# A two-layer hybrid encoder step on one core: reordering ahead of the sliding-window attention, an earlier key split, and a feed-forward loop written out

## The reference

```python
h = rms_norm(x, ln_mix)
qa, ka, va, fa, qb, kb, vb = split(h @ w_in)     # 8 heads x 64 with forgetting; 8 q / 2 kv heads x 64 windowed
logf = log_sigmoid(fa + b_f)                     # decay per head: cumsum(logf)
o = concat(fox(qa, ka, va, cumsum(logf)),        # causal softmax(q k / 8 + c_q - c_k) v
           swa(rope(qb), rope(kb), vb, sinks))   # own chunk of 64 and two before it, a sink per head
x = x + o @ w_out                                # 1024 -> 1024
x = x + cross_attend(rms_norm(x), mem)           # 4 heads x 128 into 256 memory tokens
gate, val = split(rms_norm(x) @ w_up)            # 2 x 2816
x = x + (silu(causal_conv3(gate)) * val) @ w_down
```

## Time and profile before

| | |
|---|---|
| median of 3 runs | 3662.82 us (3659.05 to 3664.21) |
| profiled execution, own time | 3655.24 us |
| its span | 3653.4 us |
| mean granted TensorE clock | 0.968 of full |
| PE busy | 3391.1 us (93%) |
| DVE, POOL, ACT busy | 51%, 33%, 23% |
| HBM traffic | 46 GB/s over the span |

### The profile page before, as it was taken

The page is one execution under the profiler, slowest core; times in us unless marked ns, Lnnn a source line. Parts: engine busy times, 40 slices in busy tenths (PEclk is TensorE's granted clock), DMA queues, the critical chain, the costliest instruction groups (busy, mean ns, idle before and its releaser), DMA issues. The chain is left out here.

```text
span 3653.4 us, 52717 instructions
## 1 busy us (share of the span) xinstructions
PE 3391.1 (93%) x21112; PEld 3257.3 (89%) x21112; DVE 1879.3 (51%) x3464; ACT 835.7 (23%) x1872; POOL 1201.9 (33%) x976
## 2 busy tenths in 40 slices
PE   6999997889999999999989999979989999999997
PEld 6988897778889999999978988878888999999997
DVE  5443444777664444443644443457766443444345
ACT  4331231434320000000232322224443100000001
POOL 4113112433343333333432122124233333333331
PEclk9999998999999999999999999988999999999998
DMA  4112112111111111111121111111111111111111
GB/s 145 39 43 58 42 37 64 56 43 39 30 41 44 43 45 44 44 46 45 41 70 51 39 42 59 46 43 61 44 35 32 41 44 44 44 44 44 45 44 63
DMA packets 85396, 175.65 MB, mean 48 GB/s; under 512 B 10416, under 2 KB 13744, under 8 KB 84752
## 3 DMA queue, kind: packets, MB, share of 16 engines
q1 hardware_dynamic: 71968, 132.90, 12.8%
q10 hardware_dynamic: 13184, 39.23, 3.7%
HBM read 150.36 MB, written 16.29 MB: 46 GB/s over the span
## 5 line engine op out<-in xcount | busy, mean ns | idle before, releaser
L613 POOL TENSOR_TENSOR WH<-RAW,zero 128x512 fp32r<-128x512 f32 x484 | 544.9, 1126 | 2366.1 <-PE PS L633 2353.6
L633 PE MATMUL PS<-HH,WH 128*128 128x384 f32 (+1 forms) x3312 | 872.0, 336 | 101.3 <-POOL WL L615 19.5
L633 PE MATMUL PS<-HL,WH 128*128 128x384 f32 (+1 forms) x3312 | 853.3, 330 | 0.0
L633 PE MATMUL PS<-HH,WL 128*128 128x384 f32 (+1 forms) x3312 | 852.6, 329 | 0.0
L633 PEld LDWEIGHTS PS<-HH,WH 128*128 128x128 f32 x3312 | 592.8, 190 | 123.4 <-POOL WL L615 22.5
L615 POOL TENSOR_TENSOR WL<-RAW,WH 128x512 fp32r<-128x512 f32 x484 | 661.4, 1367 | 37.9
L633 PEld LDWEIGHTS PS<-HL,WH 128*128 128x128 f32 x3312 | 595.4, 190 | 0.0
L633 PEld LDWEIGHTS PS<-HH,WL 128*128 128x128 f32 x3312 | 592.8, 189 | 0.0
L1686 DVE TENSOR_TENSOR XT<-PS,XT 128x320 f32<-128x320 f32 x448 | 303.3, 719 | 269.5 <-PE PS L633 269.3
L633 PE MATMUL PS<-G0H,WH 128*128 128x384 f32 (+1 forms) x960 | 288.1, 349 | 45.4 <-DVE XT L1530 29.4
L1115 ACT ACTIVATE PTH<-PS 128x512 fp32r<-128x512 f32 (+4 forms) x320 | 165.5, 520 | 681.3 <-PE PS L633 680.2
(11 more groups left out here) (249 smaller groups left out, 5087.9 us busy)
## 6 DMA issues: line engine op xcount, KB each, us to landing
RAW<-in_slabs SPq DMA_DIRECT2D x484, 256.0 KB, 2.7
XR<-decays ACTq DMA_DIRECT2D x16, 512.0 KB, 5.8
XT<-in_xT SPq DMA_DIRECT2D x8, 544.0 KB, 8.1
XR<-decays ACTq DMA_DIRECT2D x16, 272.0 KB, 7.0
out_fk<-T ACTq DMA_DIRECT2D x8, 544.0 KB, 2.7
out_fv<-T ACTq DMA_DIRECT2D x8, 544.0 KB, 2.8
out_y<-YT ACTq DMA_DIRECT2D x8, 544.0 KB, 3.2
RX<-ST ACTq DMA_DIRECT2D x16, 136.0 KB, 2.4
```

Of the source, the lines that this page charges most:

```text
L613: pool.tensor_tensor(WH[:, s, :], RAW[:, s, :], zero[:, 0:1].to_broadcast([128, HALF]), ALU.add).then_inc(w_hi, 1)
L633: ins = pe.matmul(*a, **k)
```

## The change

It has these parts.

1. At a layer's start VectorE evicts key pair 0 before it waits for `ln_done`, and ScalarE copies `KH` right after the log-sigmoid, ahead of the decay transfers. `FZ` and `FA` move to the place of `QH` and `QL`.
2. The squares of the memory tokens (layer 0) become one ScalarE instruction and one `tensor_reduce` on VectorE in place of 8 and 7.
3. Ahead of the sliding-window run the projections go query 1, values, query 2, query 3, with the value transposes in two halves behind query 2 and query 3. The first half of ("out", 1), output tiles 0 to 3, is a block of its own (`down`) before the run. The other 12 parts go one to a step into gaps 0 and 2 of steps 0 to 11. All rotary embeddings are done before the run, each after the eviction of a projection and not before it; all but query 0's swaps go through `RX`, and VectorE copies `XKL` in place of ScalarE.
4. The feed-forward loop is a Python loop, so the five turns are straight code. `repeat`, `Silent` and `wait_apart` are gone, with the constant waits of each group and step; one wait on `const_ok` stays.

```diff
-    order += [("wq", 1), ("wq", 2), "wv", ("wq", 3), ("win", 0), ("out", 1, 0), ("out", 1, 1), ("win", 1)]
+    order += [("wq", 1), "wv", ("wq", 2), ("wq", 3), ("out", 1, 0), ("win", 0), ("out", 1, 1), ("win", 1)]
@@ swa_fill
-            fox, own = down_parts(("out", 1), G_ROWS), down_parts(("out", 2), WINDOW_ROWS)
+            fox, own = down_parts(("out", 1), G_ROWS)[12:], down_parts(("out", 2), WINDOW_ROWS)
-            fill = {-1: spread(fox[:1], (2,)), 11: spread(fox[-1:], (0, 1, 2))}
-            fill |= {s: spread(fox[2 * s + 1:2 * s + 3], (0, 1, 2)) for s in range(11)}
+            fill = {s: spread(fox[s:s + 1], (0, 2)) for s in range(12)}
@@ TensorE
                 project(pe, ("wq", 1), HH, HL, CH)
+                own = project(pe, "wv", HH, HL, CH)
                 project(pe, ("wq", 2), HH, HL, CH)
-                own = project(pe, "wv", HH, HL, CH)
+                value_tiles(pe, T32, V_GROUPS[:2], own_values, own)
                 project(pe, ("wq", 3), HH, HL, CH)
+                value_tiles(pe, T32, V_GROUPS[2:], own_values, own)
                 pe.wait_ge(o_free, place.at("step", 1))
-                attention(pe, swa_steps(), swa_fill(), {-1: lambda: value_hook(pe, own)})
+                down(pe, G_ROWS, [("out", 1, 0)])
+                attention(pe, swa_steps(), swa_fill(), {})
...
-                repeat(pe, place, (FT // 2 - 1) // 2, mixer)
+                for turn in range((FT // 2 - 1) // 2):
+                    mixer(pe, turn)
@@ ScalarE, layer start
                 act.activation(FA[:], FA[:], ACT.Ln, bias=one[0:8, :]).then_inc(ln_done, 1)
+                filled(act)
+                hi(act, [(KH[:], T32[:])])
@@ ScalarE, ahead of the run
                 hi(act, [(KH[:], XR[:, 2, :])])
+                filled(act)
+                rope_swap(act, STAGES[0], 0)
                 act.wait_ge(roped, place.at("rope", 2))
                 hi(act, [(QH[:], QLS)])
...
+                filled(act)
+                act.wait_ge(roped, place.at("rope", 3))
+                rope_swap(act, STAGES[1], 0)
+                value_groups(act, V_GROUPS[:2], own_rows)
+                filled(act)
+                act.wait_ge(roped, place.at("rope", 4))
+                rope_swap(act, STAGES[2], 0)
+                for h in range(2):
+                    ins = copy(act, XKH[64 * h:64 * h + 64], KH[64 - 64 * h:128 - 64 * h, :])
+                ins.then_inc(keys_ready, 1)
+                value_groups(act, V_GROUPS[2:], own_rows)
...
                 window_queries(1)
                 window_queries(2)
+                window_queries(3)
@@ VectorE, layer start
+                fill(dve, T32)
                 dve.wait_ge(ln_done, place.at("layer", 1))
...
-                fill(dve, T32)
                 keys()
@@ VectorE, ahead of the run
                 rope(dve, T32[:], 0, 0, XR[:, 2, :])
+                fill(dve, STAGES[0], stored=False)
                 rope(dve, QLS, 1, 0, QLS)
                 lo(dve, [(KL[:], XR[:, 2, :], KH[:])]).then_inc(low_keys, 1)
                 wait_own(dve, lo(dve, [(QL[:], QLS, QH[:])]))
                 sample_queries(dve, *WINDOW_Q[0])
-                fill(dve, STAGES[0], stored=False)
+                fill(dve, T32)
+                place.add("store")
                 rope(dve, STAGES[0], 0, 1, STAGES[0])
                 fill(dve, STAGES[1], stored=False)
-                rope(dve, STAGES[1], 1, 1, STAGES[1])
-                fill(dve, T32)
-                place.add("store")
+                value_groups(dve, V_GROUPS[:2], own_rows)
+                rope(dve, STAGES[1], 0, 2, STAGES[1])
                 dve.wait_ge(k32_out, place.at("layer", 16, 16))
                 fill(dve, STAGES[2], stored=False)
+                dve.wait_ge(low_keys, place.at("layer", 1))
+                for h in range(2):
+                    ins = dve.tensor_copy(XKL[64 * h:64 * h + 64], KL[64 - 64 * h:128 - 64 * h, :].bitcast(F32))
+                ins.then_inc(keys_ready, 1)
+                value_groups(dve, V_GROUPS[2:], own_rows)
+                add_out(dve, 0)
                 low_queries(1)
-                wait_own(dve, low_queries(2))
+                add_out(dve, 1)
+                low_queries(2)
+                add_out(dve, 2)
+                rope(dve, STAGES[2], 0, 3, STAGES[2])
+                add_out(dve, 3)
+                wait_own(dve, low_queries(3))
...
-                hooks |= {4: lambda: rope(dve, STAGES[2], 0, 2, STAGES[2]), 5: lambda: low_queries(3)}
-                hooks[-1] = own_values
@@ the memory tokens' squares
-                for m in range(KT):
-                    act.activation(MSQ[m][:], MR[:, m, :], ACT.Square).then_inc(msq_ready, 1)
+                act.activation(MSQ[:, :, :], MR[:, :, :], ACT.Square).then_inc(msq_ready, 1)
...
+                dve.tensor_reduce(MACC[:], MSQ[:].rearrange("p k n -> p n k"), mybir.AxisListType.X, ALU.add).then_inc(msq_used, 1)
```

More of the change, by code:

```diff
@@ L11 @@
-from contextlib import ExitStack, contextmanager
+from contextlib import ExitStack
 import numpy as np
@@ L66, in __init__ @@
         self.n = dict.fromkeys(self.KINDS, 0)
-        self.loops = []
     def at(self, kind, more=0, scale=1):
[L70 to L74, removed]
+        return self.n[kind] * scale + more
     def bank_set(self):
@@ L79, in set_count @@
     def set_count(self, more=0):
[L80 to L84, removed]
-    def uses_of(self, s, more=0):
[L88 to L92, removed]
+        return self.n["use"] // 2 + more
+    def uses_of(self, s, more=0):
+        return (self.n["use"] + 1 - s) // 2 + more
     def add(self, kind, k=1):
         self.n[kind] += k
[L98 to L132, removed]
 def slab_places():
@@ L745, in down @@
                 slots = None
-                for m in range(KT):
+                for m in range(4 * len(keys)):
                     s = claim(pe)
@@ L904, in scores @@
                     qh, ql = WINDOW_Q[st["pair"]]
-                    pe.wait_ge(keys_ready, place.at("layer", 2, 2))
+                    pe.wait_ge(keys_ready, place.at("layer", 3, 3))
                     for h in range(2):
@@ L915, in scores @@
                     kv = st["pair"] // 2
-                    pe.wait_ge(keys_ready, place.at("layer", 1, 2))
+                    pe.wait_ge(keys_ready, place.at("layer", 1, 3))
                     product(o + KEEP, DEC, QSH[:], QSL[:], KSH[:, kv, :], KSL[:, kv, :])
@@ L1306, in biases, with keys @@
                         act.dma_start(XR[64 * h:64 * h + 64, 2, :], row[:, SEQ:N_C8].to_broadcast([64, T])).then_inc(bias_in, 16)
-                def keys(pair, ready):
-                    ready(act)
+                def keys(pair):
+                    parts_filled(act)
                     hi(act, [(KH[:], T32[:])])
@@ L1316, in trig, with own_rows @@
                     act.dma_start(XR[:, 1, :], sin_t).then_inc(trig_in, 16)
+                def own_rows(tile):
+                    return 128 if tile < NB else DEC
                 biases(0)
-                keys(0, filled)
+                store_t32(act, o_fk[l * PAIRS], 0, T)
                 filled(act)
@@ L1377, in window_queries @@
                     hi(act, [(WINDOW_Q[p][0], STAGES[p - 1])])
-                filled(act)
                 window_queries(1)
                 window_queries(2)
-                for out, src in ((XKH, KH), (XKL, KL)):
-                    for h in range(2):
-                        ins = copy(act, out[64 * h:64 * h + 64], src[64 - 64 * h:128 - 64 * h, :])
-                ins.then_inc(keys_ready, 1)
+                window_queries(3)
+                place.add("use", KT // 2)
+                place.add("third", KT // 2)
                 def memory_tokens():
@@ L1450, in mixer @@
                         down(act)
-                repeat(act, place, (FT // 2 - 1) // 2, mixer)
+                for turn in range((FT // 2 - 1) // 2):
+                    mixer(act, turn)
                 act.dma_start(o_cv[l], CO[:]).then_inc(co_out, 16)
@@ L1632, in attention @@
                             waits.append((p_used, place.at("step", s + 1)))
-                        wait_apart(dve, memset_ok, 4, waits)
+                        for produced in waits:
+                            dve.wait_ge(*produced)
                         if st["kind"] == "swa":
@@ L1871, in mixer @@
                         down(dve)
-                repeat(dve, place, (FT // 2 - 1) // 2, mixer)
+                for turn in range((FT // 2 - 1) // 2):
+                    mixer(dve, turn)
                 if l < DEPTH - 1:
```

57 lines of the change are left out of this document (26 added, 31 removed).

## The result

The changed kernel takes 3581.15 us (median of 4 runs, 3576.0 to 3587.93), the kernel before 3661.03 (4 runs): ratio 0.9783, 95% interval 0.9767 to 0.9799, 79.9 us less. Its profiled execution has a span of 3574.2 us, 79.2 less than that of before; the mean granted clock rose from 0.968 to 0.977. The forecast was 3587, range 3569 to 3609.

What follows compares the result with a forecast made beforehand. It took TensorE as the bound, busy 3391.1 of 3653.4 us, gains coming only from idle time and half clock; -22.0 - 36.4 - 15.5 - 2 = -75.9 from 3655.24, plus 7.6 for the median: 3587 us, range 3569 to 3609.

Steps and rivals of the forecast that it cites:

- Feed-forward, -15.5: Feed-forward loop: the jump back idles TensorE 1.8 us at each of 8 returns, plus 1.1; straight code saves 15.5 us.
- rival 2: Feed-forward loop: the gap is GpSimd's weight split and stays at every turn; +15.5 us, about 3602, chance 0.07.
- Rival 5: Written-out turns: straight code pauses for instruction fetch, making the kernel slower, 3677 at five pauses a turn; chance 0.02.
- Layer start, -22.0: Layer starts: early key eviction ends the key stall and half clock behind it; gains 11.1 and 11.9, less 1.0 us.
- Must find the key store landed: Layer starts: the earlier value eviction needs the key store landed; 1.0 us charged over both layers with the broadcasts' lateness.
- while that gap holds: Layer start: the 2.5 us memory-square reduction between query 0 and value eviction costs nothing, 2 us if twice as long.
- Rival 3: Layer starts: decays become the bound, first step waits for broadcasts and store; up to 6 us a layer, 3598, chance 0.06.
- Ahead of the run: Entry to sliding-window run: 7.36 us stall goes, block stalls 2.9 and 3.8; step 0 at 618.6, before 617.66.
- Steps 0 to 11, with the clock: Sliding-window run: twelve steps in 49.2 us plus 4.5 for the clock, before 72.8; gain 18.2 a layer.
- TensorE still sets it: Steps of the sliding-window run: one part fewer each; TensorE, at 4.0 us against VectorE's 3.4, sets the pace; 4.1 taken.
- Rival 1: Sliding-window run: block stalls keep the clock at half into first steps; 7 to 9 us a layer back, 3603, chance 0.14.
- Constant waits, -2: Forgetting attention's steps: removing constant waits saves some 0.05 us each where VectorE sets the pace; -2 us, bounds 0 and -10.

Runs made afterwards that it cites:

- experiment 1: Kernel before with only the feed-forward loop written out as straight code: 3641.21 us against 3654.31, ratio 0.9966.
- experiment 5: Changed kernel with each layer's first key store issued ahead of the decay transfers: 3572.2 us, ratio 0.9765 to the kernel before.
- experiment 6: As experiment 5, with layer 0's reduction of the memory squares moved behind the query eviction: 3573.91 us, ratio 0.9767 to the kernel before.
- experiment 7: Changed kernel with the last rotary embedding put back into the run at step 4: 3579.95 us, ratio 0.9795 to the kernel before.
- after_again: The changed kernel, unaltered, timed again beside experiment 11 on one chip: 3574.76 us, ratio 0.978 to the kernel before.
- Experiment 8: Changed kernel without the block, all 24 output projection parts back in the run: 3603.09 us, ratio 0.9861 to the kernel before.
- experiment 4: Kernel before with only the constant waits of each group and attention step removed: 3656.58 us against 3654.31, ratio 1.0006.
- experiment 9: Changed kernel with the whole output projection (8 tiles) as the block, no parts in steps 0 to 11: 3564.78 us, ratio 0.9755 to the kernel before.
- experiment 11: Changed kernel with the edits of experiment 5, experiment 6 and experiment 9 together: 3556.53 us, ratio 0.972 to the kernel before.
- experiment 2: Kernel before with only the layer-start parts, keys evicted ahead of the decays and memory squares merged: 3635.05 us against 3654.31, ratio 0.9957.

## Why the prediction was right, and where it was not

The time lies 6 us below the forecast, within the range, and every part but the constant waits has its sign. By its steps:

- **Feed-forward, -15.5**: measured 16.3, and 16.4 alone (experiment 1). Right, with its reason; rival 2 is refuted. The Trainium skill's rule on taken branches (Runtime: NRT & Kernel Launch, section "Instruction fetch mechanics") agrees with it; what each of the 1.34 to 1.84 us at a return is made of no run shows. Rival 5 didn't happen: no pause lies inside the written-out turns.
- **Layer start, -22.0**: measured 18.5 by the stages. The value evictions come 6.5 and 7.4 us earlier from the norm, together 13.9; the other 4.9 of layer 1 aren't shown to be the change's, since the kernel before has a stretch of 13.7 us at half clock in its attention there (from 2050) that the changed one lacks. Two terms failed. "Must find the key store landed" was charged with 1.0 us and cost 5: the store is issued behind 1.6 MB of broadcasts and lands 11.1 us after its issue. Ahead of them it lands after 3.3 us (experiment 5), and the evictions come 1.1 and 3.9 us earlier. The reduction was put at nothing, "while that gap holds", and cost 2.9 in layer 0 (experiment 6): it took 3.80 us where 2.5 was the estimate. Rival 3 had named the resource and was right in part: 4.6 and 4.5 us a layer are missing of its "up to 6", but the tail was taken as the broadcasts' and was the store's.
- **Ahead of the run**: step 0 at 70.5 us behind the stage's mark, before 69.8; forecast 0.9 later. The block's waits 1.67 and 3.65 against 2.9 and 3.8. The first is right with its reason. The second has the right size, but its last releaser was GpSimd's split (experiment 7), which the forecast put at nothing; VectorE's eviction, which it named, was nearly as late. That is in part luck.
- **Steps 0 to 11, with the clock**: 52.7 and 50.7 against 53.7. The sum is right because two errors cancel. Step 0 takes VectorE only 0.4 us, not 4.1, since VectorE came late and found no wait for step 1's scores. Steps 7 to 11 take 23.7 us, 4.7 each, where 4.1 was forecast because "TensorE still sets it": TensorE is busy for 19.3 of these 23.7 us and VectorE for 18.0, and the parts still wait for `XT` evictions. The six steps between take 28.6 and 26.7 us, against 24.6 and the 4.5 charged for the clock.
- **Rival 1** came as a sign and not as a price. The half clock does reach into the first steps: 13.7 us from 610.9 and 10.2 us from 2375.6, where the kernel before has 20.5 and 23.9, and the granted clock near 0.67 that the prediction named as a sign of being wrong is there in layer 0. The 7 to 9 us a layer didn't follow. That sign couldn't tell the cases apart.
- **Behind step 12**, where the forecast had nothing, a further 1.7 and 1.5 us came. With the steps that makes 43.7 for 36.4. In three other kernels with the same code in the run (experiments 5, 6 and `after_again`) it is 41.0, 40.8 and 45.8.
- **The reason given for the run was incomplete.** The prediction said that a stall goes and that a dozen parts move ahead. Experiment 8 shows that without the block the order would have opened a wait of 14.90 us. The sum was right because it walked TensorE through the block second by second and so saw VectorE's 16 us; a reader who takes only "the stall is removed" would expect the gain without the block too.
- **Constant waits, -2**: nothing (experiment 4).

**What stays open.** The parts alone sum to 0.34 + 0.43 + 1.05 - 0.06 = 1.76% by their ratios, the whole is 2.17% (2.01 to 2.33). Between steps 12 and 35 the changed kernel takes 118.0 and 117.4 us, the kernel with the window part alone 120.4 and 120.4; both have the same work there. That the constant waits are the difference is unlikely: experiment 4 is no faster there without them, and without them experiment 7 takes 117.8 us in one layer and 119.8 in the other. Why the stretches at half clock fall as they do wasn't tried.

## What to carry to other kernels

When an order is changed to remove a stall, write down what the other engine does in one piece afterwards, and put matmuls that ask little of it beside that piece: here the block was worth 21.0 us of the run's stages, and the order with its early embeddings 22.7 without it. A move that ends a wait exposes the next user of the same buffer, so follow the buffer's store through its DMA queue, behind everything issued ahead of it. And a releaser in a row is only the last event before the idle time ended. Check it at a second place with the same dependences, and look how long before the matmul it ended: in this case 0.05 us where TensorE waited for the split, 0.3 to 0.8 us where it didn't. A sum that comes out right should be taken apart too: here 53.7 for 52.7 hid two errors of over 3 us each.

## What the runs showed that was not expected

- Two scans of VectorE on 8 partitions took 3.05 and 1.20 us after the change, 2.25 and 0.34 before, with GpSimd's splits now at the same time.
- The half clock behind a short wait varies between executions of the same code, from 6.8 to 17.1 us behind the value groups of pair 0 in layer 1. The first stage of layer 0, with the same code, took 498.2 us in `after_again` and 505.1 in experiment 8, and the run stages of experiments 9 and 11 differ by 3.5 and 3.9.
- Not all half clock follows a wait. In five of the fourteen profiled executions (`before`, experiments 1, 2, 4 and 8) there is one stretch of 13.7 us at half clock inside a forgetting attention, and in the 10 us ahead of it TensorE is recorded busy without a break. In the kernel before (windows, columns as in the earlier trace rows):

```profile
2040.30:2050.30 10.00, 10.00 (x73) 8.72 (x72) 5.62 (x16) 4.39 (x12) 0.00 (x0) 1.00 0.01 2
2050.30:2064.00 13.70, 13.70 (x59) 12.83 (x59) 5.29 (x14) 4.00 (x11) 0.00 (x0) 0.50 0.00 1
```

- A gain of 4 us at layer 1's first eviction (experiment 5) reached the next stage as 0.6 us.
